# Norms by halves of 256 tokens across a stage's joint, and all eight sums of squares on TensorE

## The reference

```python
for l in range(DEPTH):
    x = x + 0.5 * m[2] * swiglu(modulate(rmsnorm(x, norm_w[l, 0]), m[0], m[1]), ffn1_w13[l], ffn1_w2[l])
    h = modulate(rmsnorm(x, norm_w[l, 1]), m[3], m[4])
    y, yc = mixer(h, hc, w_in[l], ...)          # window attention and gated linear attention, then w_out
    x = x + m[5] * y
    x = x + 0.5 * m[8] * swiglu(modulate(rmsnorm(x, norm_w[l, 2]), m[6], m[7]), ffn2_w13[l], ffn2_w2[l])
```

## Time and profile before

| | us |
|---|---|
| median of 3 runs (lowest, highest) | 2396.04 (2395.38, 2396.58) |
| the profiled execution | 2396.47 |
| its span, first to last instruction | 2394.6 |
| TensorE busy in it | 2295.2 (96%) |
| VectorE busy | 1368.7 (57%) |
| ScalarE busy | 886.2 (37%) |

### The profile page before, as it was taken

One profiled execution on the slowest core, in us unless ns is written; L12 is line 12 of the kernel. 1 busy time (PEld: TensorE's weight loads), 2 busy tenths in 40 slices (PEclk: granted clock), 3 DMA queues, 4 the chain that ended last, 5 costly groups with the idle time before them and its releaser, 6 DMA issues.

```text
span 2394.6 us, 29354 instructions
## 1 busy us (share of the span) xinstructions
PE 2295.2 (96%) x12273; PEld 1938.4 (81%) x12273; DVE 1368.7 (57%) x1780; ACT 886.2 (37%) x1280; POOL 180.9 (8%) x253
## 2 busy tenths in 40 slices
PE   6999999998999999999999999999999989999998
PEld 3888887777788888788888868878878778889998
DVE  4778722466466464476652277785146646566554
ACT  3322212454544354332222142222135535554442
POOL 0000000000133340000000000000000033230000
PEclk8999999999999999999999999999999999999999
DMA  8666532220221212345542346673323222335663
GB/s 287 190 197 195 187 106 88 71 72 25 82 66 58 89 59 82 116 143 164 182 135 99 95 126 191 191 216 138 106 71 107 70 89 89 106 97 156 188 185 132
DMA packets 298251, 302.05 MB, mean 126 GB/s; under 512 B 7392, under 2 KB 268488, under 8 KB 297096
## 3 DMA queue, kind: packets, MB, share of 16 engines
q1 hardware_dynamic: 297696, 300.00, 40.0%
q10 hardware_dynamic: 424, 0.18, 0.0%
HBM read 299.10 MB, written 1.05 MB: 125 GB/s over the span
## 4 chain that ended last, share of the span: by engine, by line
PE 85%; DVE 7%; ACT 3%; issue 2%; DMA 1%; SPq 1%; POOL 1%; DVEq 0%; ACTq 0%
PE PS L1363 25%; PE PS L1364 24%; PE PS L1365 24%; DVE WL L900 2%; PE PS L1501 1%; PE PS L1806 1%; PE PS L1747 1%; PE PS L1440 1%; PE PS L1441 1%; PE PS L1442 1%; PE PS L1758 1%; PE PS L1643 1%; PE PS L1700 1%; PE PS L1467 1%; DVE small L1097 1%
## 5 line engine op out<-in xcount | busy, mean ns | idle before, releaser
L1363 PE MATMUL PS<-hH,WH 128*128 128x512 f32 (+1 forms) x2096 | 763.1, 364 | 15.8 <-DVE hL L969 15.1
L1364 PE MATMUL PS<-hL,WH 128*128 128x512 f32 (+1 forms) x2096 | 751.9, 359 | 0.0
L1365 PE MATMUL PS<-hH,WL 128*128 128x512 f32 (+1 forms) x2096 | 751.3, 358 | 0.0
L900 DVE TENSOR_TENSOR WL<-raw,WH 128x1024 fp32r<-128x1024 f32 x420 | 505.7, 1245 | 408.6 <-ACT WH L556 408.4
L556 ACT CAST WH<-raw 128x1024 fp32r<-128x1024 f32 x420 | 419.9, 1048 | 376.7 <-PE PS L1365 362.5
L1363 PEld LDWEIGHTS PS<-hH,WH 128*128 128x128 f32 x2096 | 398.7, 190 | 89.4 <-issue 30.6
L1365 PEld LDWEIGHTS PS<-hH,WL 128*128 128x128 f32 x2096 | 398.4, 190 | 58.4
L1364 PEld LDWEIGHTS PS<-hL,WH 128*128 128x128 f32 x2096 | 399.0, 190 | 56.9 <-issue 1.2
L925 DVE SCALAR_TENSOR_TENSOR mraw<-mraw,cst 128x1024 f32<-128x1024 f32 x224 | 274.2, 1280 | 18.1 <-DMA mraw<-in_w_mod 18.0
L1363 PE MATMUL PS<-hidH,WH 128*128 128x512 f32 (+1 forms) x704 | 261.3, 371 | 0.0
L1365 PE MATMUL PS<-hidH,WL 128*128 128x512 f32 (+1 forms) x704 | 255.3, 363 | 0.0
(11 more groups left out here) (197 smaller groups left out, 2711.0 us busy)
## 6 DMA issues: line engine op xcount, KB each, us to landing
raw<-in_ffn_w SPq DMA_DIRECT2D x176, 512.0 KB, 5.2
mraw<-in_w_mod SPq DMA_DIRECT2D x128, 512.0 KB, 4.7
raw<-in_w_in SPq DMA_DIRECT2D x54, 1024.0 KB, 5.3
raw<-in_ffn_w SPq DMA_DIRECT2D x44, 1024.0 KB, 4.9
raw<-in_w_branch_attn SPq DMA_DIRECT2D x8, 1024.0 KB, 5.2
raw<-in_w_branch_gla SPq DMA_DIRECT2D x8, 1024.0 KB, 5.3
raw<-in_w_out SPq DMA_DIRECT2D x8, 1024.0 KB, 5.2
mfirst_b<-in_w_mod SPq DMA_DIRECT2D x4, 1024.0 KB, 10.2
```

What stands on the lines that cost most here:

```text
L900: nc.vector.tensor_tensor(half(WL, n % 2, e, rows), half(raw, n % 2, e, rows), half(WH, n % 2, e, rows).bitcast(F32), ALU.subtract).then_i ...
L1363: mm(o, wh, ah, start=start, stop=False)
L1364: mm(o, wh, al, start=False, stop=False)
L1365: return mm(o, wl, ah, start=False, stop=stop)
```

## The change

Two parts of 256 tokens (`c` = 0 and 1) are now followed separately through each joint. `FULL[n]` says how many tiles ahead of norm `n` are still made for all 512 tokens at once (norm 0: 8, 1: 2, 2: 6, 3: 2, 4: 2, 5: 0); the others are made first for half 0 and then for half 1. `LATE[n]` names the residuals of half 1 that VectorE does inside the first half's norm. The sums of squares are made in one block per half (`sums(n, c)`): half 0 near the end of the last group or output unit, half 1 inside the next stage's first unit, behind `kt` = 4. The next stage's first unit runs alone, half 0 and then half 1; the second unit follows whole. Its cast and difference move from ahead of the norm to inside or behind the second half.

```diff
+        FULL = [KT, 2, 6, 2, 2, 0, 0]
+        LATE = [{}, {1: 6, 2: 7}, {0: 6, 5: 7}, {1: 6, 2: 7}, {1: 6, 2: 7}, {}]
+        SS = (1, 3)
```

ScalarE's `norm(n)`:

```diff
+                for kt in range(FULL[n]):
+                    if j != 2:
+                        square(n, kt)
+                for kt in range(KT - 2 if j == 2 else FULL[n], KT):
+                    square(n, kt, 0)
+                if n and two:
+                    for kt in range(FULL[n], KT):
+                        if kt not in LATE[n].values():
+                            square(n, kt, 1)
...
+                log(0)
+                root(0)
                 if n == 0:
+                    log(1)
+                    root(1)
                     prep(0)
                     prep(1)
                 for kt in range(KT):
+                    if kt in LATE[n]:
+                        square(n, LATE[n][kt], 1)
+                    high(kt, 0)
+                    if n and two and kt == 5:
+                        log(1)
+                    if n and two and kt == 6:
+                        root(1)
+                if n:
+                    prep(second, only=0)
+                if two:
+                    for kt in range(KT // 2):
+                        high(kt, 1)
+                if n:
+                    prep(second, only=1)
+                if two:
+                    for kt in range(KT // 2, KT):
+                        high(kt, 1)
```

VectorE's `norm(n)` (`scaled` writes `sq`, `low` writes `hL`):

```diff
+                dve.wait_ge(rstd_done, 2 * n + 1)
+                for kt in range(KT):
+                    scaled(kt, 0)
+                    if kt:
+                        low(kt - 1, 0)
+                    if kt in late:
+                        residual(n, late[kt], 1)
+                low(KT - 1, 0)
+                if not two:
+                    prep(second)
+                    return
+                dve.wait_ge(rstd_done, 2 * n + 2)
+                for kt in range(KT):
+                    scaled(kt, 1)
+                    if kt:
+                        low(kt - 1, 1)
+                    if n and kt == KT // 2:
+                        prep(second, only=0)
+                low(KT - 1, 1)
                 if n:
-                    prep(next_units(n)[1])
+                    prep(second, only=1)
```

TensorE's first unit behind a norm, and its sums:

```diff
+            def first_unit(norm, step):
+                n, cs = next_units(norm)[0], norm_tokens(norm) // S
                 pe.wait_ge(lo_ready, 2 * n + 2)
-                for kt in range(KT // 2):
-                    pe.wait_ge(h_ready, KT * norm + kt + 1)
-                    first(n, kt)
-                    if kt == 0:
-                        pe.wait_ge(lo_ready, 2 * n + 4)
-                    second(n + 1, kt)
...
+                for c in range(cs):
+                    for kt in range(KT):
+                        pe.wait_ge(h_ready, norm_at(norm, kt, c))
+                        step(n, kt, c, c == cs - 1 and kt == KT - 1)
+                        if norm and c < cs - 1 and kt == KT // 2:
+                            sums(norm, 1)
...
+            def sums(n, c):
+                own = slice(c * S, (c + 1) * S)
+                for kt in range(KT):
+                    pe.wait_ge(sq_done, half_at(n, kt, c))
+                    ins = mm(PS[:, SS[c], own], ones[:], sq[:, kt, own], start=kt == 0, stop=kt == KT - 1)
+                ins.then_inc(ss_done, 1)
```

TensorE's last output group of `ffn(k)`, for the three stages with a norm behind them:

```diff
+                for m in range(FULL[norm]):
+                    for e in range(2):
+                        ins = down(g, e, m)
+                    ins.then_inc(y_done, 1)
+                for c in range(2):
+                    for m in range(FULL[norm], KT):
+                        if c:
+                            pe.wait_ge(x_ready, half_at(norm, m, 0))
+                        for e in range(2):
+                            ins = down(g, e, m, c * S, (c + 1) * S)
...
+                        if c and m == FULL[norm] + 1:
+                            sums(norm, 0)
```

TensorE's last unit of the output projection of layer 0 (in layer 1 the unit stays whole, and all eight sums follow it):

```diff
+                for c in range(2):
+                    own = slice(c * S, (c + 1) * S)
+                    for m in range(2):
...
+                        for kt in range(KT):
+                            ins = mm3(PS[:, 6 + m, own], wh[:, kt, m * P:(m + 1) * P], wl[:, kt, m * P:(m + 1) * P],
+                                      mH[:, kt, own], mL[:, kt, own], kt == 0, kt == KT - 1)
+                            if c and m == 0 and kt == KT // 2:
+                                sums(3 * l + 2, 0)
```

More of the change, by code:

```diff
@@ L357, in mod_sums, with norm_tokens, halves, half_at @@
             return mraw[:, 1, c * D:(c + 1) * D]
+        FULL = [KT, 2, 6, 2, 2, 0, 0]
+        LATE = [{}, {1: 6, 2: 7}, {0: 6, 5: 7}, {1: 6, 2: 7}, {1: 6, 2: 7}, {}]
+        SS = (1, 3)
+        def norm_tokens(n):
+            return T2 if n < 5 else S
+        def halves(n):
+            cs = range(norm_tokens(n) // S)
+            return [(kt, c) for kt in range(FULL[n]) for c in cs] + [(kt, c) for c in cs for kt in range(FULL[n], KT)]
+        def half_at(n, kt, c):
+            return sum(len(halves(m)) for m in range(n)) + halves(n).index((kt, c)) + 1
+        def norm_at(n, kt, c):
+            return KT * (2 * n + c) + kt + 1
         def next_units(n):
@@ L571, in norm @@
+            def norm(n):
                 l, j = divmod(n, 3)
-                second = next_units(n)[1]
+                second, two = next_units(n)[1], norm_tokens(n) == T2
                 nc.scalar.preload_act_table_set(LN_EXP)
[L574 to L580, removed]
@@ L885, in _ @@
                 out_proj(l)
-                norm(3 * l + 2, tokens(2 * l + 1))
+                norm(3 * l + 2)
                 ffn(2 * l + 1)
@@ L893, in _, with prep @@
         def _(dve):
-            def prep(n, rows=False):
+            def prep(n, rows=False, only=None):
                 if n >= N_UNITS:
                     return
-                for e in range(2):
+                for e in range(2) if only is None else (only,):
                     dve.wait_ge(hi_ready, 2 * n + e + 1)
@@ new lines, in norm, with scaled, low @@
+            def norm(n):
+                l, j = divmod(n, 3)
+                second, two = next_units(n)[1], norm_tokens(n) == T2
+                shift = modcol(l, 3 * j)
+                def scaled(kt, c):
+                    own = slice(c * S, (c + 1) * S)
+                    nc.vector.scalar_tensor_tensor(sq[:, kt, own], xT[:, kt, own], coefA[:, kt, c:c + 1], rstd[:, own],
+                                                   ALU.mult, ALU.mult).then_inc(xn_done, 1)
+                def low(kt, c):
+                    own = slice(c * S, (c + 1) * S)
+                    dve.wait_ge(h_hi, norm_at(n, kt, c))
+                    nc.vector.scalar_tensor_tensor(hL[:, kt, own], sq[:, kt, own], shift[:, kt, c:c + 1],
+                                                   hH[:, kt, own].bitcast(F32), ALU.add, ALU.subtract).then_inc(h_ready, 1)
+                dve.wait_ge(coef_ready, n + 1)
+                late = LATE[n]
+                dve.wait_ge(rstd_done, 2 * n + 1)
[17 more added lines that the diff above has]
+                low(KT - 1, 1)
+                if n:
+                    prep(second, only=1)
@@ L1341, in _ @@
                 ffn(2 * l)
-                norm(3 * l + 1, T2)
+                norm(3 * l + 1)
                 attn_proj(l)
@@ L1551, in ffn @@
                 ins.then_inc(half_done, 2)
-                for g in range(1, GROUPS):
+                for g in range(1, GROUPS - (k < 3)):
                     pe.wait_ge(hid_lo, g0 + g + 1)
@@ L1622, in attn_proj @@
                 swaps(4)
-                sums(5)
+                qk_sums(5)
                 scores(l, 0)
```

251 lines of the change are left out of this document (131 added, 120 removed).

## The result

| | us |
|---|---|
| before, median of 7 runs (lowest, highest) | 2396.04 (2394.11, 2397.12) |
| after, median of 7 runs (lowest, highest) | 2402.25 (2398.02, 2404.43) |
| ratio, 95% interval | 1.0026 (1.0015 to 1.0037) |
| the profiled execution of after, its span | 2401.7, 2399.8 |

The change makes the kernel slower by 0.26%. Run again later beside another set of runs of before, the ratio was 1.0020 (1.0011 to 1.0029). The forecast was 2398.3, with a range of 2390 to 2404.

The account below looks back on a forecast made before the run. TensorE, busy 2295.2 of 2394.6 us, was taken as the bound. Terms: start -0.2, joints 1, 3, 4 +1.8 +1.7 +1.7, joint 2 -2.6, joint 5 -0.9, half clock +0.8: +2.3 on 2396.04, so 2398.3 us, range 2390 to 2404.

Parts of the forecast that it names:

- line of 4.8 us: Whole kernel: a smaller change counts as the same; chances faster 0.14, same 0.55, slower 0.31.
- rival B: Slower: half clock at joints 1, 3, 4 and 5 not hidden, 1.5 us each, 2403.5 us; chance 0.25.
- Joints 1, 3 and 4: Norms into attention (1, 4) and feed-forward (3): 48.9 us each, losing 1.8, 1.7 and 1.7, half clock aside.
- Joint 2: Norm after the output projection: first wait and its half clock gone, 44.4 us against 47.0, 2.6 gained.
- Joint 5: Norm into a feed-forward block, 256 tokens only: 25.0 us against 25.9, 0.9 gained.
- The start: Joint 0: first `hL` 1.2 us earlier, clock low before and after, end 0.2 us earlier.
- Splitting: Each 512-column matmul cut in two costs 0.013 us more; 300 make 3.9 us, contained in the joint sums.
- Half clock: TensorE at 1.2 GHz behind first waits, mostly hidden: 0.2 us at each of joints 1, 3, 4, 5; 0.8 in all.
- bound of 0.85 us per joint: Half-clock cost at joints 1, 3, 4 and 5 from which rival B decides.
- A: Faster: late squares and second logarithm don't hold up the stream; 19.0 us of waits go, 2379.3 us; chance 0.14.
- C: At joints 1, 3 and 4 TensorE still waits 4.3 us, 2.0 more at each, 2404.3 us; chance 0.06.
- half-clock stretches follow each joint as before: One of the signs in the changed profile that would show the prediction wrong.

Follow-up runs that it names:

- e1: Changed kernel with ScalarE doing each late square behind its step's shift instead of ahead of it; 2394.4 us, ratio 0.9992.
- e2: Changed kernel with the second unit's casts and differences moved beside the second sums at joints 1 to 4; 2396.4 us, ratio 0.9997.
- e3: Changed kernel with half 1's logarithm and exponential behind all eight shifts of half 0 at joints 1 to 4; 2398.8 us, ratio 1.0010.
- e8: Kernel before the change with 294 of its 512-column matmuls cut into two of 256 columns each; 2401.8 us, ratio 1.0021.
- e9: The changed kernel run once more without an edit; 2401.6 us, ratio 1.0020.
- e4: Changed kernel with norms 1, 3 and 4 put back as in the kernel before; 2389.0 us, ratio 0.9969.
- e5: Changed kernel with the three moves together, the edits of e1, e2 and e3; 2386.4 us, ratio 0.9959.
- e6: Changed kernel with 12, 6 and 6 unread matmuls ahead of the first unit's steps 0, 1 and 2 at joints 1, 3 and 4; 2398.9 us, ratio 1.0009.
- e7: Kernel of e5 with 12 unread matmuls ahead of step 0 at joints 1, 3 and 4; 2384.5 us, ratio 0.9953.
- e10: Kernel before the change with 17 unread 512-column matmuls in the 4.3 us wait at joints 1, 3 and 4; 2391.3 us, ratio 0.9981.

## Why the prediction was right, and where not

The time lies in the range, but the forecast of +2.3 us was far off: +6.2 and, in the later run, +5.7. By the prediction's own line of 4.8 us both are slower, which had 0.31, and not the same, which had 0.55. The range held because it took in all of rival B.

- **Joints 1, 3 and 4, the order.** Forecast 48.9 us with all waits, measured 48.6 at full clock. Right, 0.3 too much, of which the 36 splits at 0.011 instead of 0.013 are 0.1. Each wait was then taken away by moving the entry that was named for it: the late square (e1), the weight difference (e2), the second logarithm (e3).
- **Joint 2.** Forecast 44.4 and no first wait; 44.1 and none. The half clock there went with the wait, as forecast. What the prediction didn't see is that this is the whole gain: by the estimate above the old order takes 44.1 too at full clock, since the short waits and the splits take back what the wait gave.
- **Joint 5.** Forecast 25.0, measured 25.0, with a first wait of 2.75 and 0.66 for the second unit's weights.
- **The start**, by the end of its second unit (68.47 to 67.03 us). Forecast -0.2, measured -1.4 in after's first trace, -0.6 to +0.3 in the traces of e1 to e3, which have the same start. The clock is low there for 10 to 17 us, and what it does moves the start by more than the code does; the 1.4 can't be put down to the change.
- **Splitting.** 0.013 us each against 0.011 measured (e8). The formula of the Trainium skill ("TensorE: Matmul & The Clock Gate", Back-to-back issue gap) has 2.5 ns for each matmul, and the section says that it holds for a matmul by itself and counts too little for small ones that come with a weight load. An estimate by it is 0.1 us for the 42 splits of joint 1; 0.43 was measured (e8). Here the rows were the better guide.
- **Half clock: the step that was mis-sized.** I took 0.2 for each of joints 1, 3, 4 and 5, 0.8 in all, "the steps at which it would fall are the 1.83 us ones, which hide it". Measured: 1.8 and 1.6 at joints 3 and 4 of after's profile, none at 1 and 5, 3.4 in all; in its second profile (e9) 0.6, 1.8 and 1.7 at joints 1, 3 and 4, and some 0.2 at 5. The mechanism was read rightly as far as it went: at steps 1 and 2 it is hidden. But the stretch at joints 3 and 4 is 6.8 us long, not 3.4, and so reaches over step 2's end and steps 3 and 4, which nothing hides. The earlier trace rows had shown such a stretch of 6.9 us at joint 2; the prediction had the longer case as a bound, twice 1.5 us, and put nothing of it into the sum.
- **Rival B** named just this, at 1.5 us for each of four joints and 2403.5. It gave the bound of 0.85 us per joint from which it decides; 3.4 over four joints is exactly that, and the medians, 2402.3 and 2401.6, lie nearer to it than to the forecast.
- **Rivals A and C.** A falls: the late squares and the second logarithm do hold up the stream (e1, e3). Its terms add up to 18.6 us, not 19.0, which would have made it 2379.7. C falls: the first wait is 2.2 us, not 4.3.
- **Of what would show it wrong**, that "half-clock stretches follow each joint as before" is half met: joints 1, 2 and 5 have lost theirs in the first trace, 3 and 4 have kept theirs and at 4 it is longer; in the second trace only joint 2 is without.

The sum against the profiled spans (+5.2): the order at joints 1, 3 and 4 +4.1 (forecast 5.2), joint 2 -2.8 (-2.6), joint 5 -0.9 (-0.9), half clock +3.4 (0.8), the rest +1.4 (-0.2), which the experiments show to be within its spread.

One thing I had not priced at all: how much of before's joints was half clock. Only with it do the two orders compare. Filled, the old order takes 45.7, 45.0 and 45.7 us at joints 1, 3 and 4, the new one 48.6 at each. The halved first wait gave 2.1 us, and 5.0 to 5.7 went elsewhere: five short waits with 3.7 us in the trace's column and 0.16 more for each by starts, steps that follow VectorE at 0.80 us instead of TensorE at 0.72, and splits (0.4 us at joints 1 and 4, 0.9 at joint 3, which is why joint 3 lost the most). At joint 2 the first half's sum lies far enough ahead of TensorE's last work for the whole chain of the norm to be hidden, and the two orders come out alike; with the three moves the new one takes 42.0, 2.1 less by the estimate.

What stays open: what made the 4.3 us of e4 outside the joints, and whether the three moves are worth more than norms 1, 3 and 4 left in the old form. Without half clock the two differ by under 0.5 us a joint, and no run put them side by side with the waits of both filled.

## What to carry to other kernels

Halving a norm takes TensorE's wait away where TensorE has work left that covers the whole chain (joint 2), and halves it elsewhere. Either way the second half's squares, logarithm and weight preparation can land between the shifts and writes of `hL` that TensorE is following: here a late square delayed it by 0.6 us, the logarithm by 0.9 and a weight difference by 1.1, and together with the splits they took back at least what the shorter wait gave. Place such entries where the engine that carries them is idle anyway, here beside the second sums. And before comparing two orders by a trace, take out the half clock: where TensorE stands idle and dense work follows, as behind the waits of 2.2 and 4.3 us here, some matmuls without a reader in the wait are worth trying.

## What the runs showed of the hardware

- Behind the first waits of joints 1, 3 and 4 the granted clock fell to the 1.2 GHz level in 21 of 27 cases in the nine traces in which TensorE stood idle there: in 12 of 18 behind 2.2 us (after, e1, e2, e3, e5, e9) and in all 9 behind 4.2 to 4.3 us (before, e4, e8), for 3.4 or 6.8 us. With TensorE's own unread matmuls in the wait it fell in none of 9 (e6, e7, e10). The same kernel met it differently in two traces (joint 1: none in after, 3.4 us in e9), so a difference of 1 to 2 us at one joint of one trace says little.
- A half-clock stretch of 6.8 us cost joints 3 and 4 of after 1.8 and 1.6 us, though matmuls ran at half speed through nearly all of it: the short waits swallow the rest. In the old order, which has no waits behind the first, 4.7 us of work under the half level cost 2.2 (joint 3).
- Under the half level a 256-column matmul starts every 0.213 us, a 512-column one every 0.427, at the full one every 0.120 and 0.227 (before, after, e9).
- Seventeen 512-column matmuls fitted into a wait of 4.3 us, and the first useful one still waited 0.32 us for `hL` (e10).
